# First expert blocks split among the pool chunks, norm sums two chunks at a time, third tile's rows turned behind the gather

## The chip, the core and the metric

The kernel runs on one core of one Trainium2 chip. The metric is the device time of one execution in microseconds (us). Four compute engines work beside one another, each in the order of its own program: PE (TensorE, matrix products, with the weight loads PEld beside them), DVE (VectorE), ACT (ScalarE) and POOL (GpSimd). SP issues most of the DMA transfers. They wait for one another on semaphores.

## The reference, cut to what matters

One inference step of a two-layer decoder over 280 tokens (16 meta tokens, 256 prompt tokens, 8 sample tokens), width 1024. Layer 0 is a state-space and sparse-attention mixer and a dense SwiGLU. Layer 1, where the change lies, is:

```python
def pool_mixer(u, hist, pos0, pool_w, pool_scale):      # windows 2, 4, 8, 16, one for each quarter of the channels
    ...
        mean = (cg - lagged)[:, n_hist:] / jnp.minimum(float(w), pos + 1.0)[None, :, None]
        pooled.append(mean - ext32[:, n_hist:, sl])
    mixed = jnp.einsum('bsgc,gcd->bsgd', pooled, pool_w.astype(f32)).reshape(B, S, D_MODEL)
    return (mixed * pool_scale.astype(f32)).astype(u.dtype), ext[:, T - POOL_HIST:]

def moe(h, router_w, w_gate, w_up, w_down):
    logits = (t @ router_w).astype(jnp.float32)
    top_v, top_i = lax.top_k(logits, TOP_K_EXPERTS)      # 2 of 8
    gates = jax.nn.softmax(top_v, axis=-1)
    ...
        out = out + dense_gate[:, e:e + 1] * swiglu(t, w_gate[e], w_up[e], w_down[e]).astype(jnp.float32)

def odd_layer(x, ...):
    y, new_hist = pool_mixer(rmsnorm(x, norm_mix), hist, pos0, pool_w, pool_scale)
    x = x + y
    x = x + moe(rmsnorm(x, norm_ffn), router_w, w_gate, w_up, w_down)
```

## The kernel before

The activations lie with channels on the partitions: 8 chunks (`c`) of 128 channels by 280 tokens (`x3` the residual, `h3` the normed rows). The program of every engine is written out by hand in this order: mixer, dense layer, **pool stage**, **router**, **gather**, and then a loop of passes, one for each expert (8 here, more if an expert has over 128 tokens).

**Pool stage.** DVE forms the sums over each window by doubling (L2215), two chunks at a time (group g = 0 to 3), writes mean minus token to `pl` (L2217 for the 272 prompt tokens, L2220 and L2221 for the first few, L2222 and L2223 for the 8 sample tokens) and counts `pooled`. PE multiplies each group by `pool_w` (L1233, two output chunks a group; each fp32 product is two records in the trace). DVE adds the result to the residual (`add_mixed`, L2205). ACT then scales the chunk by the next norm's weight into `h3` (L1707) and squares it into `sqs` (L1708). PE sums each chunk for the router's logits (L1217) and for the norm (L1221): that is `last_norm_sums`. Before, chunks 0 to 3 are summed after output chunk 5 of the pool product, and chunks 4 to 7 after chunk 7.

**Router.** ACT takes the root of the norm sums (`root(3)`, L1437) and copies the logits out (L1723). PE turns the rows of `h3` to tokens on partitions (`token_rows("h2n", ...)`, L1246), the norm (L1254) and the logits (L1259). DVE picks the two experts of a token (L2242 to L2265, which counts `picked`), and PE counts the rank of each token in its expert (L1267). DVE makes from it the selection matrices `pick` (L2281).

**Gather.** PE turns the residual's rows for the output (`token_rows("xn", ...)`, L1246, three token tiles of 128, 128 and 24; ACT copies each to `acc`, L1441), gathers the tokens of the first expert (L1277), fills two banks with zeros (`y`, L1302) and begins the passes.

**Expert weights.** A pass has 84 blocks of 128 x 1024. SP loads them in halves of 1 MB (two blocks) into `raw_w`. A block is split into a high part, copied by ACT (`high_part`, L1718), and a low part, subtracted by DVE (`low_part`, L2235), in one of 7 places. PE does three products a column range (L1322, L1326, L1327). ACT and DVE prepare blocks five ahead (`AHEAD`). Before the loop, ACT splits blocks 0 to 2 behind the root and 3 and 4 behind the router's rows; DVE subtracts blocks 0 and 1 (`FIRST_LOW = 2`) ahead of the router's arithmetic and 2 to 4 behind the gather. SP's half 7 waits for two low parts, half 8 for four, and so on.

PE's results go to seven banks in rotation (`fill_order` gives the order of fills, and so the bank of each); a fill waits until the last user of its bank has emptied it.

Of the kernel before, what the change touches and what calls it, by code (L numbers as in the profile page):

```python
# [24 lines left out]
P = 128  # L25
# [55 lines left out]
def shape_constants():  # L81
# [32 lines left out]
    for g, w in enumerate(WINDOWS):  # L114
        put("rw")[:, g * 16:g * 16 + w - 1] = 1.0 / np.arange(1, w, dtype=np.float32)
# [54 lines left out]
def fill_order():  # L170
# [33 lines left out]
    f += [("pool", c) for c in range(C)] + ["norm3"]  # L204
    f += ["router", ("h2n", 0, 0), ("h2n", 0, 1), "stdT", "routerT"] + [("h2n", t, i) for t in (1, 2) for i in range(2)]
    f += ["rank"] + [("xn", t, i) for t in range(TC) for i in range(2)]
# [76 lines left out]
FIRST_HIGH, FIRST_LOW = 3, 2  # L283
# [9 lines left out]
def hybrid_step(nc, a, o):  # L293

    with ExitStack() as ctx:
# [171 lines left out]
        win_a = tk(C * NP_).rearrange("p (c t) -> p c t", c=C)  # L467
        win_b = tk(C * NP_).rearrange("p (c t) -> p c t", c=C)
# [6 lines left out]
        ext = low[:, 2 * C * NP_:2 * C * NP_ + C * NB * 16].rearrange("p (c b r) -> p c b r", c=C, b=NB)  # L475
        pnew = low[:, FT * T + C * T + 2 * T:FT * T + C * T + 2 * T + D]
        assert 2 * C * NP_ + C * NB * 16 <= FT * T and D <= 4 * T
# [243 lines left out]
        def _(pool):  # L721
# [105 lines left out]
            for i in range(2):  # L827
                emptied(pool, ("xn", 2, i))
            nc.gpsimd.memset(pickTr[:, :].bitcast(F32), 0.0)
            nc.gpsimd.memset(ybr[:, :].bitcast(F32), 0.0).then_inc(sem("late_zeros"), 1)  # L830

        @block.tensor
        def _(pe):
# [367 lines left out]
            for i in range(2):  # L1201
                out = open_fill(("pnew", i))
                for q in range(4):
                    last = nc.tensor.transpose(out[0:23, q * P:(q + 1) * P], h3[:, 4 * i + q, T - 23:T], ident)
                last.then_inc(full(("pnew", i)), 1)
# [4 lines left out]
            def last_norm_sums(c0, c1):  # L1210
# [4 lines left out]
                for c in range(c0, c1):  # L1215
                    pe.wait_ge(sem("mixed_scaled"), c + 1)
                    last = mm(ps("router")[0:NE, 0:T], rw[:, c, :], h3[:, c, :], start=(c == 0), stop=(c == C - 1))  # L1217
                    if c == C - 1:
                        last.then_inc(full("router"), 1)
                    pe.wait_ge(sem("squares"), 3 * C + c + 1)  # L1220
                    last = mm(ps("norm3")[:, 0:T], ones, sqs[3][:, c, :], start=(c == 0), stop=(c == C - 1))  # L1221
                    if c == 0:

                        last.then_inc(sem("blocks_begun"), PLACES)
                    if c == C - 1:
                        last.then_inc(full("norm3"), 1)

            for co in range(C):
# [6 lines left out]
                last.then_inc(full(("pool", co)), 1)  # L1235
                if co == 5:
                    last_norm_sums(0, 4)
# [27 lines left out]
            for t in range(TC + 1):  # L1265
                for u in range(min(t + 1, TC)):
                    last = mm(out[:, t * NE:(t + 1) * NE], const("tri") if u == t else ones, sel[:, u, :],  # L1267
                              start=(u == 0), stop=(u == min(t, TC - 1)))
            last.then_inc(full("rank"), 1)
            token_rows("xn", x3, range(TC))  # L1270
# [23 lines left out]
            for half in range(2):  # L1294
                b = PASS_BANK[("gather", half)]
                pe.wait_ge(bank_free[b], BEFORE_FILL[b])
                gather_half(half, bank[b])
            pe.wait_ge(sem("late_zeros"), 1)
            for half in range(2):
                b = PASS_BANK[("y", half)]  # L1300
                pe.wait_ge(bank_free[b], BEFORE_FILL[b])
                mm(bank[b][:, :], yb3[:, 0, 0:P], yb3[:, 0, 0:512], start=True, stop=True).then_inc(bank_full[b], 1)  # L1302
# [117 lines left out]
        def _(act):  # L1420
# [284 lines left out]
            for c in range(C):  # L1705
                emptied(act, ("pool", c))
                A(h3[:, c, :], x3[:, c, :], ACT.Identity, scale=param("g_ffn1")[:, c:c + 1]).then_inc(sem("mixed_scaled"), 1)  # L1707
                A(sqs[3][:, c, :], x3[:, c, :], ACT.Square).then_inc(sem("squares"), 1)  # L1708
            root(3)

# [9 lines left out]
            for n in range(FIRST_HIGH):  # L1720
                high_part(0, n)
# [11 lines left out]
            for n in range(FIRST_HIGH, AHEAD):  # L1733
                high_part(0, n)
            act.wait_ge(sem("router_gap"), 1)
            A(g12[:, 1, :], g12[:, 0, :], ACT.Exp).then_inc(sem("router_exp"), 1)
            for t in range(TC):
                for i in range(2):
                    filled(act, ("xn", t, i))
                    n = TCN[t]  # L1740
                    copy_out(("xn", t, i), acc[0:n, t, i * 512:(i + 1) * 512], ps(("xn", t, i))[0:n, :])
            for half in range(2):
# [3 lines left out]
                  ACT.Copy).then_inc(sem("high_copied"), 1)  # L1746

# [64 lines left out]
        def _(dve):  # L1812
# [395 lines left out]
            for g, w in enumerate(WINDOWS):  # L2208
# [3 lines left out]
                for k in range(g + 1):  # L2212
                    dst, n = window_home(k)[:, cs, :], 1 << k
                    nc.vector.tensor_copy(dst[:, :, 0:n], src[:, :, 0:n])
                    link(TT(dst[:, :, n:NP_], src[:, :, n:NP_], src[:, :, 0:NP_ - n], ALU.add))  # L2215
                    src = dst
                link(STT(pl[:, cs, 0:NP_], win[:, cs, :], 1.0 / w, h3[:, cs, 0:NP_], ALU.mult, ALU.subtract))  # L2217

                few = const("rw")[:, g * 16:g * 16 + w - 1].unsqueeze(1).to_broadcast([P, 2, w - 1])
                link(TT(pl[:, cs, 0:w - 1], win[:, cs, 0:w - 1], few, ALU.mult))  # L2220
                link(TT(pl[:, cs, 0:w - 1], pl[:, cs, 0:w - 1], h3[:, cs, 0:w - 1], ALU.subtract))  # L2221
                link(nc.vector.tensor_reduce(pl[:, cs, NP_:T], ext[:, cs, :, 16 - w:16], AX.X, ALU.add))  # L2222
                STT(pl[:, cs, NP_:T], pl[:, cs, NP_:T], 1.0 / w, h3[:, cs, NP_:T], ALU.mult,  # L2223
                    ALU.subtract).then_inc(sem("pooled"), 1)
# [269 lines left out]
```

## Time and profile before

| | us |
|---|---|
| median of 3 runs | 1585.21 |
| lowest and highest run | 1580.08, 1591.72 |
| the profiled execution: its own time | 1590.82 |
| its span in the profile | 1588.7 |

Of the span PE is busy 97%, DVE 82%, ACT 62%, POOL 7%. A row of the time line gives start, busy time, engine, line, operation, output<-input, shapes and count, and in brackets how long the engine had been idle before it and what ended that. A row of the stretches gives the stretch, its length, the busy time of each engine in it with the number of instructions, TensorE's granted clock (1.00 is 2.4 GHz, 0.50 is 1.2 GHz), the DMA engines' busy share and GB/s.

### The profile page before, as it was taken

What the parts mean: (1) busy time and instruction counts of PE and PEld (TensorE: products, weight loads), DVE (VectorE), ACT (ScalarE), POOL (GpSimd) and SP (SyncE); (2) the same over time, 40 slices, a digit from 0 to 9 for tenths busy, and PEclk for the clock granted to TensorE, in tenths of its full rate; (3) what the DMA queues carried; (4) which work ended last, traced back from release to release, by engine and by line L of the source; (5) the groups of instructions that cost most, each with busy time, mean ns of one, the idle gap of its engine ahead of it and who ended that gap; (6) DMA issues with size and microseconds to landing.
All of it is one profiled execution on the core that took longest, in us unless ns stands there. A gap on an engine that the chain in (4) does not pass through costs nothing.

```text
span 1588.7 us, 23294 instructions
## 1 busy us (share of the span) xinstructions
PE 1537.4 (97%) x7624; PEld 1236.3 (78%) x7624; DVE 1299.2 (82%) x1729; ACT 992.1 (62%) x1302; POOL 110.8 (7%) x156
## 2 busy tenths in 40 slices
PE   6999899999998899999999999999999999999998
PEld 5665464999997578888888888888888888888886
DVE  8978883666644689889889889989989989988986
ACT  5121352544432467787787777777777778777774
POOL 1277600000000000000000000000000000000000
PEclk9998887999999899999999999999999999999999
DMA  6401244454464269989989989999998998999992
GB/s 230 160 27 54 66 160 128 154 177 159 127 182 172 106 221 362 380 307 358 374 315 357 365 319 355 370 341 329 360 357 323 366 364 307 366 371 327 345 363 89
DMA packets 212891, 420.83 MB, mean 265 GB/s; under 512 B 10233, under 2 KB 56469, under 8 KB 212572
## 3 DMA queue, kind: packets, MB, share of 16 engines
q1 hardware_dynamic: 211542, 414.37, 72.6%
q10 hardware_dynamic: 622, 3.45, 0.6%
q0 software_dynamic: 672, 2.32, 0.4%
q8 instruction: 30, 0.49, 0.1%
q14 instruction: 25, 0.20, 0.0%
HBM read 417.50 MB, written 3.07 MB: 265 GB/s over the span
## 4 chain that ended last, share of the span: by engine, by line
PE 85%; DVE 3%; ACT 1%; issue 1%; SPq 0%; DMA 0%; DVEq 0%; ACTq 0%
PE bank L1327 19%; PE bank L1322 19%; PE bank L1326 19%; PE bank L1176 3%; PE bank L1180 3%; PE bank L1179 3%; PE bank L1347 2%; PE bank L1191 1%; PE bank L1195 1%; PE bank L1194 1%; PE bank L885 1%; PE bank L1285 1%; PE bank L1362 1%; DVE split L2235 1%; PE bank L1233 1%
## 5 line engine op out<-in xcount | busy, mean ns | idle before, releaser
L2235 DVE TENSOR_TENSOR split<-raw_w,split 128x1024 fp32r<-128x1024 f32 x672 | 787.1, 1218 | 42.5 <-ACT split L1718 39.1
L1718 ACT ACTIVATE split<-raw_w 128x1024 fp32r<-128x1024 f32 x672 | 688.8, 1060 | 121.2 <-PE bank L1322 119.3
L1322 PE MATMUL bank<-split,xgr 128*128 128x512 f32 x896 | 358.1, 400 | 1.1 <-DVE xgr L2302 1.1
L1327 PE MATMUL bank<-split,xgr 128*128 128x512 f32 x896 | 354.2, 395 | 0.0
L1326 PE MATMUL bank<-split,xgr 128*128 128x512 f32 x896 | 354.1, 395 | 0.0
L1327 PEld LDWEIGHTS bank<-split,xgr 128*128 128x128 f32 x896 | 169.0, 189 | 39.8
L1322 PEld LDWEIGHTS bank<-split,xgr 128*128 128x128 f32 x896 | 169.2, 189 | 39.2 <-issue 1.5
L1326 PEld LDWEIGHTS bank<-split,xgr 128*128 128x128 f32 x896 | 169.1, 189 | 37.9
L1322 PE MATMUL bank<-split,hbr 128*128 128x512 f32 x448 | 178.0, 397 | 0.0
L1327 PE MATMUL bank<-split,hbr 128*128 128x512 f32 x448 | 177.0, 395 | 0.0
L1326 PE MATMUL bank<-split,hbr 128*128 128x512 f32 x448 | 176.8, 395 | 0.0
L1176 PE MATMUL bank<-split 128*128 128x280 f32 x352 | 102.8, 292 | 0.0
L1180 PE MATMUL bank<-split 128*128 128x280 f32 x352 | 102.5, 291 | 0.0
L1179 PE MATMUL bank<-split 128*128 128x280 f32 x352 | 102.1, 290 | 0.0
L1327 PEld LDWEIGHTS bank<-split,hbr 128*128 128x128 f32 x448 | 84.2, 188 | 19.9
L1326 PEld LDWEIGHTS bank<-split,hbr 128*128 128x128 f32 x448 | 84.3, 188 | 19.3
L1322 PEld LDWEIGHTS bank<-split,hbr 128*128 128x128 f32 x448 | 84.3, 188 | 19.3
L1661 ACT ACTIVATE split<-ring 128x1024 fp32r<-128x1024 f32 x44 | 46.6, 1059 | 65.5 <-PE bank L1176 65.5
L1784 ACT ACTIVATE late<-bank 128x512 f32<-128x512 f32 x56 | 33.5, 597 | 72.4 <-PE bank L1327 72.3
L2345 DVE TENSOR_TENSOR hbr<-bank,hbr 128x512 fp32r<-128x512 f32 x56 | 38.5, 688 | 49.0 <-ACT hbr L1761 48.9
L2143 DVE TENSOR_TENSOR split<-ring,split 128x1024 fp32r<-128x1024 f32 x44 | 53.9, 1225 | 19.2 <-ACT split L1661 19.2
L1176 PEld LDWEIGHTS bank<-split 128*128 128x128 f32 x352 | 66.3, 188 | 0.0
(429 smaller groups left out, 1993.1 us busy)
## 6 DMA issues: line engine op xcount, KB each, us to landing
raw_w<-in_moe_gate SPq DMA_DIRECT2D x112, 1024.0 KB, 5.5
raw_w<-in_moe_up SPq DMA_DIRECT2D x112, 1024.0 KB, 6.0
raw_w<-in_moe_down SPq DMA_DIRECT2D x112, 1024.0 KB, 5.7
ring<-in_w_gate SPq DMA_DIRECT2D x11, 1024.0 KB, 5.0
ring<-in_w_up SPq DMA_DIRECT2D x11, 1024.0 KB, 7.4
ring<-in_w_down SPq DMA_DIRECT2D x8, 1408.0 KB, 6.8
ring<-in_w_in SPq DMA_DIRECT2D x5, 2048.0 KB, 9.4
ring<-in_w_out SPq DMA_DIRECT2D x2, 2048.0 KB, 9.0
```

The source lines that it names most:

```text
L1176: first = mm(out[:, 0:T], w[0][:, c, :], dense_in(0, c), start=(c == 0), stop=False)
L1179: mm(out[:, 0:T], w[0][:, c, :], dense_in(1, c), start=False, stop=False)
L1180: last = mm(out[:, 0:T], w[1][:, c, :], dense_in(0, c), start=False, stop=(c == C - 1))
L1322: first = mm(out, hi, place[:, s, 0, cols], start=start, stop=False)
L1326: mm(out, lo, place[:, s, 0, cols], start=False, stop=False)
L1327: last = mm(out, hi, place[:, s, 1, cols], start=False, stop=stop)
L1661: A(place[:, n % FF_PLACES, 0, :].rearrange("p (c m) -> p c m", c=C), unit(name, 256)[:, k * C:(k + 1) * C, (f % 2) * P:(f % 2) * P + P], ...
L1718: A(place[:, s, 0, :], raw_w[:, at:at + BLOCK], ACT.Copy).then_inc(sem("high_ready"), 1)
L1784: A(th[:, j % 2, :], bank[b][:, :], ACT.Silu).then_inc(bank_free[b], 1)
L2143: TT(low_, unit(f"ffn{f // 2}", 256)[:, k * C:(k + 1) * C, (f % 2) * P:(f % 2) * P + P], high.bitcast(F32), ALU.subtract).then_inc(sem("ff ...
L2235: TT(place[:, s, 1, :], raw_w[:, at:at + BLOCK], place[:, s, 0, :].bitcast(F32), ALU.subtract).then_inc(sem("low_ready"), 1)
L2345: TT(dst, src, high.bitcast(F32), ALU.subtract).then_inc(bank_free[PASS_BANK[name]], 1)
```

## The change

Five things are altered, none of them inside the loop of passes:

1. DVE's pooling writes the sample tokens' sums into the window buffer and finishes prompt and sample tokens with one instruction; the table `rw` carries the factor `w` so that the first tokens need one small product.
2. The norm sums of chunks 0 and 1 follow output chunk 3, those of 2 and 3 follow chunk 5.
3. ACT splits blocks 0 to 2 ahead of chunk 2's scaling and blocks 3 and 4 ahead of chunk 4's; DVE subtracts four blocks, not two, ahead of the router's arithmetic.
4. The rank takes 7 products instead of 9.
5. The third tile's residual rows are turned behind the gather, ACT copies them behind the gather's copies, and the zero fill of the `y` banks reads the zeroed `pickTr` instead of `ybr`, so that POOL waits only for the norm.

```diff
-    f += [("pool", c) for c in range(C)] + ["norm3"]
-    f += ["router", ("h2n", 0, 0), ("h2n", 0, 1), "stdT", "routerT"] + [("h2n", t, i) for t in (1, 2) for i in range(2)]
-    f += ["rank"] + [("xn", t, i) for t in range(TC) for i in range(2)]
+    f += [("pool", c) for c in range(4)] + ["norm3", "router"] + [("pool", c) for c in range(4, C)]
+    f += [("h2n", 0, 0), "stdT", "routerT", ("h2n", 0, 1)] + [("h2n", t, i) for t in (1, 2) for i in range(2)]
+    f += ["rank"] + [("xn", 0, 0), ("xn", 0, 1), ("xn", 1, 0), ("xn", 2, 0), ("xn", 1, 1), ("xn", 2, 1)]
...
-FIRST_HIGH, FIRST_LOW = 3, 2
+FIRST_HIGH, FIRST_LOW = 3, 4
...
-            for i in range(2):
-                emptied(pool, ("xn", 2, i))
-            nc.gpsimd.memset(pickTr[:, :].bitcast(F32), 0.0)
-            nc.gpsimd.memset(ybr[:, :].bitcast(F32), 0.0).then_inc(sem("late_zeros"), 1)
+            emptied(pool, "norm3")
+            nc.gpsimd.memset(pickTr[:, :].bitcast(F32), 0.0).then_inc(sem("late_zeros"), 1)
...
+                if co == 3:
+                    last_norm_sums(0, 2)
                 if co == 5:
-                    last_norm_sums(0, 4)
+                    last_norm_sums(2, 4)
             last_norm_sums(4, C)
...
-            for t in range(TC + 1):
-                for u in range(min(t + 1, TC)):
-                    last = mm(out[:, t * NE:(t + 1) * NE], const("tri") if u == t else ones, sel[:, u, :],
-                              start=(u == 0), stop=(u == min(t, TC - 1)))
+            for u in range(TC):
+                mm(out[:, TC * NE:(TC + 1) * NE], ones, sel[:, u, :], start=(u == 0), stop=(u == TC - 1))
+            mm(out[:, 0:TC * NE], const("tri"), sel[:, :, :].rearrange("p t e -> p (t e)"), start=True, stop=False)
+            for u in range(TC - 1):
+                for t in range(u + 1, TC):
+                    last = mm(out[:, t * NE:(t + 1) * NE], ones, sel[:, u, :], start=False, stop=(u == TC - 2))
             last.then_inc(full("rank"), 1)
-            token_rows("xn", x3, range(TC))
+            token_rows("xn", x3, (0, 1))
...
+            token_rows("xn", x3, (2,))
             pe.wait_ge(sem("late_zeros"), 1)
             for half in range(2):
                 b = PASS_BANK[("y", half)]
                 pe.wait_ge(bank_free[b], BEFORE_FILL[b])
-                mm(bank[b][:, :], yb3[:, 0, 0:P], yb3[:, 0, 0:512], start=True, stop=True).then_inc(bank_full[b], 1)
+                for k in range(2):
+                    last = mm(bank[b][:, k * 256:(k + 1) * 256], pickTr[:, 0:P], pickTr[:, 0:256], start=True, stop=True)
+                last.then_inc(bank_full[b], 1)
...
+            for c in range(C):
+                if c == 2:
+                    for n in range(FIRST_HIGH):
+                        high_part(0, n)
+                if c == 4:
+                    for n in range(FIRST_HIGH, AHEAD):
+                        high_part(0, n)
+                emptied(act, ("pool", c))
+                A(h3[:, c, :], x3[:, c, :], ACT.Identity, scale=param("g_ffn1")[:, c:c + 1]).then_inc(sem("mixed_scaled"), 1)
+                A(sqs[3][:, c, :], x3[:, c, :], ACT.Square).then_inc(sem("squares"), 1)
+            root(3)
...
+            token_copies((0, 1))
             for half in range(2):
                 b = PASS_BANK[("gather", half)]
                 act.wait_ge(bank_full[b], BEFORE_FILL[b] + 1)
                 A(xg4[:, 0, 4 * half:4 * half + 4, :], bank[b][:, :].rearrange("p (c s) -> p c s", c=4),
                   ACT.Copy).then_inc(sem("high_copied"), 1)
+            token_copies((2,))
...
+                    if k == g:
+                        nc.vector.tensor_reduce(win[:, cs, NP_:T], ext[:, cs, :, 16 - w:16], AX.X, ALU.add)
                     link(TT(dst[:, :, n:NP_], src[:, :, n:NP_], src[:, :, 0:NP_ - n], ALU.add))
                     src = dst
-                link(STT(pl[:, cs, 0:NP_], win[:, cs, :], 1.0 / w, h3[:, cs, 0:NP_], ALU.mult, ALU.subtract))
...
-                link(TT(pl[:, cs, 0:w - 1], win[:, cs, 0:w - 1], few, ALU.mult))
-                link(TT(pl[:, cs, 0:w - 1], pl[:, cs, 0:w - 1], h3[:, cs, 0:w - 1], ALU.subtract))
-                link(nc.vector.tensor_reduce(pl[:, cs, NP_:T], ext[:, cs, :, 16 - w:16], AX.X, ALU.add))
-                STT(pl[:, cs, NP_:T], pl[:, cs, NP_:T], 1.0 / w, h3[:, cs, NP_:T], ALU.mult,
-                    ALU.subtract).then_inc(sem("pooled"), 1)
+                link(TT(win[:, cs, 0:w - 1], win[:, cs, 0:w - 1], few, ALU.mult))
+                STT(pl[:, cs, :], win[:, cs, :], 1.0 / w, h3[:, cs, :], ALU.mult, ALU.subtract).then_inc(sem("pooled"), 1)
```

How the order moves on PE in the pool stage (L1233, in the changed kernel L1230, is the pool product; L1217 the logits' sum and L1221 the norm's). Before:

```order
L1233 MATMUL bank<-low,ring 128x280 x12
L1217 MATMUL bank<-hT,params 8x280
L1221 MATMUL bank<-low,consts 128x280
L1217 MATMUL bank<-hT,params 8x280
L1221 MATMUL bank<-low,consts 128x280
L1217 MATMUL bank<-hT,params 8x280
L1221 MATMUL bank<-low,consts 128x280
L1217 MATMUL bank<-hT,params 8x280
L1221 MATMUL bank<-low,consts 128x280
L1233 MATMUL bank<-low,ring 128x280 x4
```

And with the change:

```order
L1230 MATMUL bank<-low,ring 128x280 x8
L1217 MATMUL bank<-hT,params 8x280
L1221 MATMUL bank<-low,consts 128x280
L1217 MATMUL bank<-hT,params 8x280
L1221 MATMUL bank<-low,consts 128x280
L1230 MATMUL bank<-low,ring 128x280 x4
L1217 MATMUL bank<-hT,params 8x280
L1221 MATMUL bank<-low,consts 128x280
L1217 MATMUL bank<-hT,params 8x280
L1221 MATMUL bank<-low,consts 128x280
L1230 MATMUL bank<-low,ring 128x280 x4
```

Two pairs of sums have moved from behind the third pool group to between the second and the third.

On PE from the rank to the passes. Before:

```order
L1267 MATMUL bank<-late,consts 128x8 x9
L1246 MATMUL bank<-consts,xT 128x128 x16
L1246 MATMUL bank<-consts,xT 24x128 x8
L1277 MATMUL bank<-pickr,hnr 128x128 x40
L1302 MATMUL bank<-ybr 128x512 x2
```

And with the change:

```order
L1265 MATMUL bank<-late,consts 128x8 x3
L1266 MATMUL bank<-late,consts 128x24
L1269 MATMUL bank<-late,consts 128x8 x3
L1245 MATMUL bank<-consts,xT 128x128 x16
L1278 MATMUL bank<-pickr,hnr 128x128 x40
L1245 MATMUL bank<-consts,xT 24x128 x8
L1305 MATMUL bank<-pickTr 128x256 x4
```

The eight transposes of the third tile now stand between the gather and the zero fills, and the rank is two products shorter.

On ACT from chunk 6 of the pool stage to the router's exponential. Before:

```order
L1707 ACTIVATE hT<-xT,params 128x280
L1708 ACTIVATE low<-xT 128x280
L1437 ACTIVATE low<-bank,small 128x280
L1718 ACTIVATE split<-raw_w 128x1024 x3
L1723 ACTIVATE late<-bank 8x280
L1731 ACTIVATE hnr<-bank,small 128x512 x4
L1731 ACTIVATE hnr<-bank,small 24x512 x2
L1718 ACTIVATE split<-raw_w 128x1024 x2
```

And with the change, from the second set of splits on (L1716; the first three stand two chunks further ahead; L1726 and L1727 scale and square a chunk, L1441 is the root, L1730 the copy of the logits):

```order
L1716 ACTIVATE split<-raw_w 128x1024 x2
L1726 ACTIVATE hT<-xT,params 128x280
L1727 ACTIVATE low<-xT 128x280
L1726 ACTIVATE hT<-xT,params 128x280
L1727 ACTIVATE low<-xT 128x280
L1726 ACTIVATE hT<-xT,params 128x280
L1727 ACTIVATE low<-xT 128x280
L1726 ACTIVATE hT<-xT,params 128x280
L1727 ACTIVATE low<-xT 128x280
L1441 ACTIVATE low<-bank,small 128x280
L1730 ACTIVATE late<-bank 8x280
```

All five splits now stand ahead of the root, and nothing stands between the root and the copy of the logits.

## Rows read from the trace of the kernel before

**Rows 1.** Stretches: a pass (PE, PEld, DVE, ACT, POOL, clock, DMA share, GB/s)

```profile
690.00:817.00 127.00, 127.00 (x569) 103.10 (x568) 113.74 (x114) 98.87 (x108) 0.00 (x0) 1.00 0.95 348
```

**Rows 2.** Waits of the DMA queue in the passes: us in total, times, longest

```profile
SPq L679 <- DVE split L2235: 816.4, 328, 19.7
```

**Rows 3.** Time line of PE, pool stage: start, busy, line, count, idle before

```profile
516.46 6.93 PE L1233 MATMUL bank<-low,ring 128*128 128x280 f32 x16 [0.85 <-DVE low L2223]
525.28 3.58 PE L1233 MATMUL bank<-low,ring 128*128 128x280 f32 x8 [1.89 <-DVE low L2223]
...
530.22 0.64 PE L1217 MATMUL bank<-hT,params 128*8 128x280 f32 x2
...
531.46 0.64 PE L1217 MATMUL bank<-hT,params 128*8 128x280 f32 x2
...
533.84 2.05 PE L1233 MATMUL bank<-low,ring 128*128 128x280 f32 x8
```

**Rows 4.** Time line of DVE, pool stage and router

```profile
514.77 0.72 DVE L2217 SCALAR_TENSOR_TENSOR low<-low,hT 128x544 f32<-128x544 f32 x1
515.53 0.16 DVE L2220 TENSOR_TENSOR low<-low,consts 128x2 f32<-128x2 f32 x1
...
516.14 0.17 DVE L2223 SCALAR_TENSOR_TENSOR low<-low,hT 128x16 f32<-128x16 f32 x1
...
542.35 2.36 DVE L2235 TENSOR_TENSOR split<-raw_w,split 128x1024 fp32r<-128x1024 f32 x2 [5.91 <-ACT split L1718]
...
545.21 0.17 DVE L2249 TENSOR_TENSOR late<-bank,small 128x16 f32<-128x16 f32 x1
...
552.29 0.18 DVE L2277 TENSOR_TENSOR late<-late,bank 128x24 f32<-128x24 f32 x1 [0.69 <-PE bank L1267]
...
552.91 0.68 DVE L2281 TENSOR_SCALAR pickr<-consts,late 128x128 fp32r<-128x128 f32 x3
```

**Rows 5.** Time line of ACT, pool stage and root

```profile
525.59 0.53 ACT L1707 ACTIVATE hT<-xT,params 128x280 f32<-128x280 f32 x1 [3.62 <-DVE xT L2205]
...
531.47 0.53 ACT L1707 ACTIVATE hT<-xT,params 128x280 f32<-128x280 f32 x1 [4.27 <-DVE xT L2205]
...
540.88 0.49 ACT L1437 ACTIVATE low<-bank,small 128x280 f32<-128x280 f32 x1 [3.55 <-PE bank L1221]
541.27 2.94 ACT L1718 ACTIVATE split<-raw_w 128x1024 fp32r<-128x1024 f32 x3
```

**Rows 6.** Time line of PE, from the norm's turn to the passes

```profile
541.64 0.73 PE L1254 MATMUL bank<-consts,low 1*128 1x1 f32 x6
...
548.92 3.34 PE L1267 MATMUL bank<-late,consts 128*128 128x8 f32 x18
...
552.11 4.96 PE L1246 MATMUL bank<-consts,xT 128*128 128x128 f32 x24
556.82 4.66 PE L1277 MATMUL bank<-pickr,hnr 128*128 128x128 f32 x40
561.32 0.68 PE L1302 MATMUL bank<-ybr 128*128 128x512 f32 x2
563.07 0.57 PE L1322 MATMUL bank<-split,xgr 128*128 128x512 f32 x1 [1.08 <-DVE xgr L2302]
...
570.98 1.41 PE L1285 MATMUL bank<-ybr,pickTr 128*128 128x512 f32 x4 [0.52 <-DVE ybr L2345]
```

**Rows 7.** Stretches, PE alone: busy, granted clock, DMA share, GB/s

```profile
521.50:522.00 0.50, 0.50 (x2) 0.50 0.04 12
...
525.80:529.20 3.40, 3.40 (x8) 0.50 0.00 0
...
549.60:556.50 6.90, 6.90 (x35) 0.51 0.00 1
556.50:563.20 6.70, 5.62 (x48) 1.00 0.01 2
563.30:566.70 3.40, 3.40 (x9) 0.51 0.11 17
```

More of the change, by code:

```diff
@@ L114, in shape_constants @@
     for g, w in enumerate(WINDOWS):
-        put("rw")[:, g * 16:g * 16 + w - 1] = 1.0 / np.arange(1, w, dtype=np.float32)
+        put("rw")[:, g * 16:g * 16 + w - 1] = w * (1.0 / np.arange(1, w, dtype=np.float32))
     put("hmask")[:] = (p[:, None] % H == np.arange(H)[None, :])
@@ L466, in hybrid_step @@
         tk, at = carve(low, 0)
-        win_a = tk(C * NP_).rearrange("p (c t) -> p c t", c=C)
-        win_b = tk(C * NP_).rearrange("p (c t) -> p c t", c=C)
+        win_a = tk(C * T).rearrange("p (c t) -> p c t", c=C)
+        win_b = tk(C * T).rearrange("p (c t) -> p c t", c=C)
         assert at[0] <= FT * T
@@ L474, in hybrid_step @@
         assert after + 12 * T + C * NB * 15 <= UT_AT + 4 * T
-        ext = low[:, 2 * C * NP_:2 * C * NP_ + C * NB * 16].rearrange("p (c b r) -> p c b r", c=C, b=NB)
+        ext = low[:, 2 * C * T:2 * C * T + C * NB * 16].rearrange("p (c b r) -> p c b r", c=C, b=NB)
         pnew = low[:, FT * T + C * T + 2 * T:FT * T + C * T + 2 * T + D]
-        assert 2 * C * NP_ + C * NB * 16 <= FT * T and D <= 4 * T
+        assert 2 * C * T + C * NB * 16 <= FT * T and D <= 4 * T
         token_rs = rinv[:, 0:4]
@@ L1204, in _ @@
                     last = nc.tensor.transpose(out[0:23, q * P:(q + 1) * P], h3[:, 4 * i + q, T - 23:T], ident)
+                    if i == 0 and q == 0:
+                        last.then_inc(sem("blocks_begun"), PLACES)
                 last.then_inc(full(("pnew", i)), 1)
@@ L1221, in last_norm_sums @@
                     last = mm(ps("norm3")[:, 0:T], ones, sqs[3][:, c, :], start=(c == 0), stop=(c == C - 1))
-                    if c == 0:
-                        last.then_inc(sem("blocks_begun"), PLACES)
                     if c == C - 1:
@@ L1704, in _ @@
             act.dma_start(o["pool_s"][:, 14, :], pnew[15:23, :]).then_inc(sem("pool_out"), 16)
[L1705 to L1709, printed above, removed]
             def high_part(i, n):
@@ L1718, in high_part @@
                 A(place[:, s, 0, :], raw_w[:, at:at + BLOCK], ACT.Copy).then_inc(sem("high_ready"), 1)
-            for n in range(FIRST_HIGH):
-                high_part(0, n)
+            for c in range(C):
[9 more added lines that the diff above has]
+            root(3)
             filled(act, "router")
@@ L1732, in _, with token_copies @@
                       scale=token_rs[0:n, t:t + 1]).then_inc(sem("hn_high"), 1)
-            for n in range(FIRST_HIGH, AHEAD):
-                high_part(0, n)
             act.wait_ge(sem("router_gap"), 1)
             A(g12[:, 1, :], g12[:, 0, :], ACT.Exp).then_inc(sem("router_exp"), 1)
[L1737 to L1741, printed above, removed]
+            def token_copies(ts):
+                for t in ts:
+                    for i in range(2):
+                        filled(act, ("xn", t, i))
+                        n = TCN[t]
+                        copy_out(("xn", t, i), acc[0:n, t, i * 512:(i + 1) * 512], ps(("xn", t, i))[0:n, :])
+            token_copies((0, 1))
             for half in range(2):
```

## The prediction

> **What bounds the kernel now.** I read the stretches of the passes first. In a pass PE is busy 127.00 of 127.00 us at the granted clock 1.00 [rows 1], and SP's queue waits for DVE's low parts, not the reverse: 816.4 us in 328 waits [rows 2]. Eight passes are PE's own work and the change leaves their code alone, so whatever it moves lies between the pool stage and the first blocks of the first pass, some 55 us. Read next the time lines of PE, DVE and ACT there. In the pool stage PE starts at 516.46 when DVE's first group is ready, is done with two groups and then idle for 1.89 us before the third [rows 3]; from 525.28 it has no gap until the norm sums end at 540.85 (ACT's root starts at 540.88, after 3.55 us of waiting for PE [rows 5]). From there DVE's arithmetic leads, from its first product of logits at 545.21 to the rank at 552.29 and `pick` at 552.91 [rows 4]. Then PE leads again: 24 turned tiles, 40 gather products, two zero fills and the first pass's products at 563.07 [rows 6]. PE's granted clock falls to the lower level (1.2 GHz) after short gaps: 525.8 to 529.2, 549.6 to 556.5 and 563.3 to 566.7; the gather ran at the full level (2.4 GHz) [rows 7].
>
> **Pool stage.** A group ends with four small or large instructions: from 514.77 to 516.31 in the first group, 1.54 us [rows 4]. Now it is a small product (0.16 and its hand-over, about 0.2) and one instruction of 560 instead of 544 elements (about 0.75), and the reduction (under 0.2 here) lies unlinked before the last doubling: 1.54 - 0.95 - 0.1 = 0.49 saved, so PE starts at 515.97. The other three groups save about as much, and only the third's counts: it is ready at about 524.2 (before: 525.1).
> PE's two groups take 6.93 [rows 3], to 522.9. Chunk 0's and 1's sums follow. A chunk costs 1.24 us at the full clock (530.22 to 531.46 [rows 3]): 2.5 us, to 525.4, in a place where PE was idle 1.89. The third group finds its data there. At the full clock it takes 1.95 (the fourth group's row, 2.05 with the overlap [rows 3]), against 3.58 before: the gap after which the clock fell is filled, so I take the full clock. That is 527.3. Sums of chunks 2 and 3 to 529.8, the fourth group to 531.8, four more chunks to 536.8. Against 540.85 the norm ends **4.0 us earlier**. Should the third group run at the lower level still, it is 2.4.
> What hides ACT's five splits (4.9 us at 2.94 for three [rows 5]): ACT idled 3.62 before chunk 2 and 4.27 before chunk 4 [rows 5]. The first three run from 521.5 to 524.5, chunk 2 is ready at about 524.7; the next two from 526.5 to 528.5, chunk 4 at about 530. Were that cover gone, each split would delay the sums by 1 us, 5 in all. Their weights have come: the DMA engines fall from full to 0.04 busy at 521.5 [rows 7].
>
> **Root to logits.** Before: 540.88 to 545.21, 4.33 us [rows 4, 5]. ACT's logits copy stood behind 2.94 us of splits, DVE's first reciprocal behind two low parts (2.36 from 542.35 [rows 4]). Without them PE's turn of the norm ends the wait: it ends at 542.37 [rows 6], 1.5 after the root's start, and 0.45 of reciprocals and hand-over follow, with the logits' copy and turn (0.4 and 0.3) beside and just behind. I take 2.1: **2.2 saved**. DVE's four low parts (4 x 1.18) now start when the last chunk is added, at 532.3, and end at 537.0, 1.3 before the norm's turn. They open SP's halves 7 and 8 some 10 us sooner, in a stretch in which nothing else is loaded; POOL's zeros of `hnr` follow the last pool product, also earlier. Both cost nothing. Without that cover half a low part, 0.6, would show.
>
> **Logits to gather.** DVE's choice of experts and PE's start of the rank move along unchanged. The rank is 18 records in 3.34 us [rows 6], now 14: 3.34 x 4/18 = **0.7 saved**. 8 of 24 turned tiles leave: 4.96 x 8/24 = **1.65 saved** [rows 6]. This is PE's path; DVE's own reaches `pick` at 553.6 (552.91 and 0.68 [rows 4]), and since DVE's six low rows then end just before the rank (it waited 0.69 for it [rows 4]) that path saves 4.0 + 2.2 + 0.65, to 546.8, while PE's ends at 557.0 - 8.55 = 548.5. PE's still ends last, by 1.7. If PE had the full clock in rank and turns it would wait for `pick` at 546.8: 10.2 saved there instead of 8.55.
>
> **Behind the gather.** Before, PE ended the gather at about 561.4, filled zeros (0.68), idled 1.08 and began at 563.07 [rows 6], waiting for ACT's and DVE's second half. Now 8 turns of the third tile (1.25 to 1.65) and four short fills (0.7) come first, then the load of the pass count: 2.5 us after the gather where it was 1.6, **0.9 lost** (ends: 0.6 and 1.7, the 1.08 left whole). The turns fill the wait only in part and push the rest out.
> First pass: DVE has one low part left there, not three, 2.36 less [rows 4], so the 0.52 wait before the first scatter [rows 6] goes: **0.5 saved**. ACT's two copies of the third tile put its `y` copies 1.1 us later, under DVE's tables. Nine of the first products ran at the lower level, about 0.43 apart against 0.23, 3.4 us of it [rows 7]: 1.7 us to be had if the shorter gap leaves the clock up, 0 if not. Half, **0.8**.
>
> **Sum.** 4.0 + 2.2 + 0.7 + 1.65 - 0.9 + 0.5 + 0.8 = 8.95, say 9. Against the profiled execution's 1590.82 that is 1581.8. This execution is 5.6 above the median of the three runs (1585.21), so as a median: **1576**.
>
> The clock terms come from rows: the level fell with gaps of 1.89, some 2 and 1.08 us around it [rows 3, 6, 7]. The Trainium skill, page "TensorE: Matmul & The Clock Gate", section "Part 1: The HAM clock gate", has the clock fall only after a longer idle spell than any of these three, and rise under sustained activity. By that rule these short gaps would cost no clock, so filling them would give none back, and the sum would be 9 - 1.6 - 0.8 = 6.6; the trace disagrees. The page also says that the gate runs by itself, so that the same kernel meets it at other places from run to run; one profile can't show that. It speaks for the first rival below, whose price comes from rows.
>
> **Rivals.**
> *A, the gather at the lower clock (0.18).* Before, 4.96 us of turned tiles stood ahead of the gather and the level rose at 556.5, just before it [rows 6, 7]. Now a third of them is gone. For: the level came only at the end of the run. Against: the gap before the rank is the same and may fall otherwise. Price: 40 products at half rate, up to 4.4 us more, and up to 1 more in turns. 9 - 4.5 = 4.5 saved: 1581.
> *B, the passes take it back (0.10).* The DMA engines are 0.95 busy in a pass [rows 1]. If weights were the bound, an earlier start would only move the wait. Against: SP's queue waits for DVE [rows 2], PE never idles. 1585.
> *C, ACT late in the pool stage (0.06).* If its splits start late or the weights lag, chunk 2's scaling and all sums behind it slip; half of the cover gone, 2.5 us: 1579.
> *D, slower (0.04).* PE stays at the lower level from the first moved sums to the passes, because the work is now interleaved. Eight chunks' sums at twice 1.24 (+9.9), third group as before (the 1.6 gone), fourth +1.6, gather +4.4, the rest of the first four blocks +2.9: 20.4 against 9, net 11 slower, 1597. It decides once PE is at the lower level for more than about half of that work; against it, the level rose after 3.4 us of dense products at 529.2 [rows 7].
> The forecast has the rest, 0.62.
>
> **Range and chances.** The forecast's own ends are 12 saved (PE's full clock at the rank and at the first pass, 1573) and 6 saved (third group at the lower level and the hand-over dear, 1579). A and B reach to 1585. The three runs before lie 11.6 apart, 5 to 6.5 on either side of their median, which a new median may share in part: I widen to 1568 and 1587. One per cent, 16 us, is what a measurement tells from no change. A saving of 16 is beyond every case and needs the runs' scatter: 0.07. Slower by 16 needs more than D: 0.03. Within: 0.90.
>
> **What would show it.** In the changed profile: no PE gap between second and third pool group, and the third group in 2 us, not 3.6; the root starting near 537; the logits' first product 2.1 after it; a gather that starts near 548.5 and takes 4.4 us; the first pass's products 2.5 us behind the gather. A gather of 6 us or more is A. PE gaps inside a pass are B. A wait of PE for ACT's scaled chunks is C. The sum is wrong if the root starts later than 538.5, or if DVE's low parts end behind the norm's turn.

## The result and the profile after

| | before | changed |
|---|---|---|
| median, lowest to highest of 19 runs, us | 1588.22, 1580.08 to 1591.72 | 1580.78, 1570.86 to 1583.84 |
| the profiled execution's span, us | 1588.7 | 1576.5 |

The ratio of the runs is 0.9946, 95% interval 0.9932 to 0.9961: the change makes the kernel some 0.5% faster, 7.4 us between the medians. The forecast was 9 us. The median that it gave, 1576, lies 4.8 us below the measured 1580.78: 3.0 of that is the median before, 1588.22 here against 1585.21 in the three runs that the forecast had, and the rest is the smaller saving. The two spans lie 12.2 apart, more than the medians; the profiles of the experiments show how far two spans can differ.

A pass is as before; the stretches of the changed kernel (columns as in [rows 1]):

```profile
681.60:808.60 127.00, 127.00 (x569) 103.09 (x568) 113.37 (x113) 98.88 (x108) 0.00 (x0) 1.00 0.95 348
```

The time line of PE in the changed kernel's pool stage (L1230 is the pool product), to be laid beside [rows 3]:

```profile
516.33 5.52 PE L1230 MATMUL bank<-low,ring 128*128 128x280 f32 x16 [0.32 <-DVE low L2232]
521.78 0.64 PE L1217 MATMUL bank<-hT,params 128*8 128x280 f32 x2
...
524.18 2.12 PE L1230 MATMUL bank<-low,ring 128*128 128x280 f32 x8
...
529.51 0.71 PE L1230 MATMUL bank<-low,ring 128*128 128x280 f32 x2 [0.73 <-DVE low L2232]
```

The 1.89 us gap is gone, the third group takes 2.12 instead of 3.58, and there is a new wait: PE idles 0.73 us until DVE has the fourth group. The first two groups are shorter too, 5.52 us instead of 6.93 [rows 3]: the granted clock is low until about 519.4 here, and was until about 522.4. DVE's and ACT's time lines, beside [rows 4, 5]:

```profile
532.10 4.62 DVE L2243 TENSOR_TENSOR split<-raw_w,split 128x1024 fp32r<-128x1024 f32 x4
536.68 0.08 DVE L2248 MEMSET late<- 128x24 f32 x1
538.23 0.17 DVE L2250 RECIPROCAL small<-bank 128x2 f32<-128x2 f32 x1 [1.48 <-PE bank L1253]
...
538.67 0.18 DVE L2257 TENSOR_TENSOR late<-bank,small 128x16 f32<-128x16 f32 x1
...
545.10 0.18 DVE L2285 TENSOR_TENSOR late<-late,bank 128x24 f32<-128x24 f32 x1
```

```profile
521.30 2.94 ACT L1716 ACTIVATE split<-raw_w 128x1024 fp32r<-128x1024 f32 x3
524.49 0.53 ACT L1726 ACTIVATE hT<-xT,params 128x280 f32<-128x280 f32 x1 [0.25 <-DVE xT L2215]
...
525.99 1.99 ACT L1716 ACTIVATE split<-raw_w 128x1024 fp32r<-128x1024 f32 x2
529.82 0.53 ACT L1726 ACTIVATE hT<-xT,params 128x280 f32<-128x280 f32 x1 [1.84 <-DVE xT L2215]
...
536.63 0.49 ACT L1441 ACTIVATE low<-bank,small 128x280 f32<-128x280 f32 x1 [3.55 <-PE bank L1221]
```

Both sets of splits fit in ACT's idle time (0.25 and 1.84 us of it are left), and DVE's four low parts end 1.48 us before PE's turn of the norm. At 545.10 DVE goes from its own low rows to the rank without a wait. PE from there on, beside [rows 6]:

```profile
547.00 4.66 PE L1278 MATMUL bank<-pickr,hnr 128*128 128x128 f32 x40
551.50 1.04 PE L1245 MATMUL bank<-consts,xT 128*24 128x128 f32 x8
552.29 0.72 PE L1305 MATMUL bank<-pickTr 128*128 128x256 f32 x4
553.25 0.49 PE L1326 MATMUL bank<-split,xgr 128*128 128x512 f32 x1 [0.25 <-DVE xgr L2310]
```

The stretches of PE alone, columns as in [rows 7]:

```profile
521.80:528.60 6.80, 6.80 (x25) 1.00 0.01 2
543.20:546.70 3.50, 3.50 (x19) 0.51 0.00 0
547.00:551.50 4.50, 4.50 (x43) 1.00 0.02 5
553.20:558.90 5.70, 5.64 (x24) 1.00 0.00 0
```

From its start the gather is followed by the first pass after 6.25 us, exactly as before: turns and fills take the place of most of the idle 1.08 us, and 0.25 of it is left. Of the three low stretches that stood behind the second pool group [rows 7], one of 3.5 us is left. And the first pass's 24 products run at the full level with no wait before the scatter.

### The profile page after: what moved, and what is told of

Same layout as the page of the kernel before. It is cut to its first block, busy times and chain, and to the rows that moved or that the text cites. A ratio compares the mean times of both kernels' runs of the same rounds, so it can differ in the third digit from the quotient of the medians.

```text
span 1576.5 us, 23279 instructions
## 1 busy us (share of the span) xinstructions
PE 1528.1 (97%) x7622; PEld 1230.3 (78%) x7622; DVE 1297.2 (82%) x1721; ACT 991.4 (63%) x1302; POOL 109.1 (7%) x155
## 4 chain that ended last, share of the span: by engine, by line
PE 85%; DVE 3%; ACT 1%; issue 1%; SPq 0%; DMA 0%; DVEq 0%
PE bank L1331 19%; PE bank L1330 19%; PE bank L1326 19%; PE bank L1174 3%; PE bank L1178 3%; PE bank L1177 3%; PE bank L1351 2%; PE bank L1189 1%; PE bank L1193 1%; PE bank L883 1%; PE bank L1192 1%; PE bank L1286 1%; PE bank L1366 1%; PE bank L1110 1%; PE bank L1154 1%
## 5 line engine op out<-in xcount | busy, mean ns | idle before, releaser
L2243 DVE TENSOR_TENSOR split<-raw_w,split 128x1024 fp32r<-128x1024 f32 x672 | 787.1, 1218 | 36.6 <-ACT split L1716 32.6
L1716 ACT ACTIVATE split<-raw_w 128x1024 fp32r<-128x1024 f32 x672 | 688.2, 1060 | 118.5 <-PE bank L1326 116.6
L1326 PEld LDWEIGHTS bank<-split,xgr 128*128 128x128 f32 x896 | 168.8, 188 | 37.9 <-issue 0.4
L1665 ACT ACTIVATE split<-ring 128x1024 fp32r<-128x1024 f32 x44 | 46.6, 1059 | 65.5 <-PE bank L1174 65.5
```

The lines of the kernel that those rows point to most:

```text
L1326: first = mm(out, hi, place[:, s, 0, cols], start=start, stop=False)
L1665: A(place[:, n % FF_PLACES, 0, :].rearrange("p (c m) -> p c m", c=C), unit(name, 256)[:, k * C:(k + 1) * C, (f % 2) * P:(f % 2) * P + P], ...
L1716: A(place[:, s, 0, :], raw_w[:, at:at + BLOCK], ACT.Copy).then_inc(sem("high_ready"), 1)
L2243: TT(place[:, s, 1, :], raw_w[:, at:at + BLOCK], place[:, s, 0, :].bitcast(F32), ALU.subtract).then_inc(sem("low_ready"), 1)
```

## Experiments

Each kernel was timed in five rounds beside the kernel before on the same chip. The first four experiments below were timed together on one chip, the next four (router gap, pool wait, both, before with its gap filled) on another and the last four (both filled again, splits back with gaps filled, pooling back, rank back) on a third. Besides the ratio, every profile gives the same six times: the starts of the root of the last norm, of DVE's first product of logits, of PE's gather, of the first pass and of its fifth block (block 4), counted from the start of DVE's reciprocal of the third norm, just ahead of the pool stage; and the rest, from block 4 to the end of the span. In us:

| kernel | root | logits | gather | pass | block 4 | rest | ratio to before (95%) |
|---|---|---|---|---|---|---|---|
| before | 32.6 | 37.0 | 48.6 | 54.8 | 64.0 | 1016.5 | |
| changed | 28.0 | 30.0 | 38.4 | 44.6 | 51.5 | 1016.4 | 0.9946 (0.9932 to 0.9961) |
| changed, again | 27.9 | 29.9 | 38.7 | 49.8 | 57.1 | 1015.3 | 0.9938 (0.9918 to 0.9957) |
| norm sums back | 29.4 | 31.4 | 39.4 | 48.5 | 55.0 | 1016.4 | 0.9964 (0.9948 to 0.9980) |
| splits back | 27.9 | 32.2 | 42.2 | 53.4 | 61.7 | 1016.4 | 0.9999 (0.9983 to 1.0015) |
| turns back | 27.8 | 29.8 | 40.4 | 47.0 | 53.8 | 1016.5 | 0.9944 (0.9924 to 0.9963) |
| router gap filled | 27.9 | 29.9 | 37.9 | 44.2 | 51.1 | 1016.5 | 0.9931 (0.9908 to 0.9954) |
| pool wait filled | 27.1 | 29.2 | 37.2 | 43.8 | 50.7 | 1016.5 | 0.9929 (0.9906 to 0.9952) |
| both filled | 27.1 | 29.2 | 37.2 | 43.5 | 50.3 | 1016.4 | 0.9926 (0.9902 to 0.9949) |
| both filled, again | 28.1 | 30.1 | 38.1 | 44.4 | 51.3 | 1016.5 | 0.9929 (0.9907 to 0.9951) |
| before, gap filled | 31.0 | 35.3 | 45.3 | 51.6 | 60.7 | 1016.5 | 0.9996 (0.9978 to 1.0014) |
| splits back, gaps filled | 28.4 | 32.8 | 40.8 | 49.9 | 58.4 | 1016.4 | 0.9962 (0.9946 to 0.9979) |
| pooling back | 30.0 | 32.1 | 40.1 | 46.4 | 53.2 | 1016.5 | 0.9953 (0.9934 to 0.9972) |
| rank back | 27.9 | 29.9 | 39.5 | 46.6 | 53.4 | 1016.4 | 0.9944 (0.9924 to 0.9964) |

Each row is one profile, except that the ratio comes from all its runs. The rest is the same within 1.2 us in all: the passes take nothing back and give nothing. The reciprocal itself starts at 500.7 to 510.2 us of the span in these profiles, whatever the kernel: much of the scatter of the runs arises ahead of the stage that was changed.

**The changed kernel again** (no edit).

> The changed kernel once more, unaltered, as the yardstick of this chip. Work theory (the gain is work taken off the path that ends the stage, the same in every execution): root about 4.2 us earlier, logits' first product 2.3 us nearer to the root, gather start 3.3 us nearer, in the profile again; ratio to the kernel before 0.995. Clock theory (most of the profile's 12 us is where the clock happened to fall): the profile shows another sum, between 7 and 12 us, with the difference in stretches of granted clock 0.50; the ratio is the same 0.995.

Measured: ratio 0.9938. Up to the gather it is the same profile to 0.3 us. The gather is not:

```profile
545.36 8.78 PE L1278 MATMUL bank<-pickr,hnr 128*128 128x128 f32 x40
553.94 1.91 PE L1245 MATMUL bank<-consts,xT 128*24 128x128 f32 x8
```

```profile
517.60:541.20 23.60, 20.97 (x101) 1.00 0.48 173
541.30:558.20 16.90, 16.90 (x78) 0.50 0.01 1
```

40 products take 8.78 us instead of 4.66, in a stretch in which the rows show PE busy all the time and the granted clock is 0.50. That is the first rival of the prediction, in the same kernel that did not show it in the other profile. Up to the start of the gather the work theory holds; from there to block 4 the same program took 13.1 us in one execution and 18.4 in the other.

**Norm sums back.**

```diff
-                if co == 3:
-                    last_norm_sums(0, 2)
                 if co == 5:
-                    last_norm_sums(2, 4)
+                    last_norm_sums(0, 4)
```

> The changed kernel with the norm sums of chunks 0 to 3 together behind output chunk 5, as before; all else as changed. Work theory: PE idles some 2.2 us ahead of the third pool group and the two chunks' sums (2.5 us) come behind it; root start against the third norm's root 1.4 us later than in the changed kernel. Clock theory: the gap also lets the clock fall, the third group takes 3.6 us and not 2.1, root 3 us later.

```profile
524.74 2.13 PE L1230 MATMUL bank<-low,ring 128*128 128x280 f32 x8 [2.33 <-DVE low L2230]
```

Root 1.4 us later, as the work theory has it. A gap of 2.33 us stands before the third group and the clock did not fall after it: a gap of that length did not lower it every time. In the runs the loss is 3.8 us between the medians (1581.62 and 1577.80), more than the 1.4 of the path, with intervals that overlap; this profile's gather ran in part at 0.50.

**Splits back** (ACT's five `high_part` behind the root and behind the router's rows, and no longer among the chunks; `FIRST_LOW = 2`).

```diff
-FIRST_HIGH, FIRST_LOW = 3, 4
+FIRST_HIGH, FIRST_LOW = 3, 2
...
             root(3)
+            for n in range(FIRST_HIGH):
+                high_part(0, n)
```

> The changed kernel with ACT's five splits behind the root and behind the router's rows, and DVE's two low parts ahead of the router, as before. Work theory: root start unchanged, the logits' first product 4.3 us behind the root's start and not 2.0 (2.3 us lost), and 0 to 0.5 us of wait before the first scatter: 2.3 to 2.8 us slower in all. Rival (the splits were hidden and DVE's choice of experts or PE sets the end anyway): under 0.5 us slower.

The path is as expected: logits 4.3 behind the root, 2.3 lost. But the kernel lost all that the change had gained: its median is 1587.76 us, the changed kernel's in the same rounds 1577.80 and the kernel before's 1587.62. Its profile:

```profile
540.67 0.37 PE L1258 MATMUL bank<-consts,late 8*128 8x8 f32 x3 [2.25 <-ACT late L1726]
```

```profile
540.10:563.50 23.40, 22.32 (x104) 0.50 0.14 46
```

The clock is low from PE's wait for the copy of the logits (2.25 us) until into the first pass, and the gather takes 8.8 us. Both theories I had for this kernel were too small for the 10 us; it led to the filled gaps.

**Turns back** (`token_rows("xn", x3, (0, 1, 2))` ahead of the gather and ACT's copies with it).

> The changed kernel with the third tile's rows turned and copied ahead of the gather, as before. As predicted (turns ahead cost 1.65, behind they cost 0.9 of it again): 0.8 us slower. As the changed profile reads (the first pass began 1.6 us behind the gather in both, so behind the gather the turns were free): 1.0 to 1.6 us slower. Clock theory: PE's gap behind the gather is again over 1 us, the clock falls with it and the first 9 products take 0.43 us apart: up to 3.4 us slower.

```profile
547.61 1.49 PE L1245 MATMUL bank<-consts,xT 128*24 128x128 f32 x6
548.75 5.01 PE L1278 MATMUL bank<-pickr,hnr 128*128 128x128 f32 x40
553.60 0.68 PE L1304 MATMUL bank<-pickTr 128*128 128x256 f32 x4
555.36 0.50 PE L1325 MATMUL bank<-split,xgr 128*128 128x512 f32 x1 [1.07 <-DVE xgr L2308]
```

The gather starts 1.7 to 2.0 us later and the 1.07 us gap behind it is back. Against the changed kernel's first profile the first pass and block 4 come 2.3 us later, more than the 1.0 to 1.6: the turns are 2.0 of it, and the gather, whose start still ran at the lower level, takes 5.01 us instead of 4.66. The clock theory's part missed: after the 1.07 us gap the clock did not fall, and the first products ran at the full level. In the timing (0.9944 against 0.9938 in the same rounds) no difference shows.

**Idle products on PE.** These kernels add products of constants that no result uses, into a bank that is overwritten afterwards. The one for the router's gap, ahead of the last turned rows:

```diff
+                if i == 1:
+                    for _k in range(2):
+                        mm(filler[:, 0:512], ones, consts[:, 0:512], start=True, stop=True)
                 out = open_fill(("h2n", 2, i))
```

> The changed kernel with two more products on PE (128 x 512, fp32, constants only, into the bank that the rank overwrites) in the 1.9 us in which PE waits ahead of the last turned rows and the rank. No result uses them. Clock theory (that gap lets the clock fall, and then rank, turns and in some executions the gather run at the lower level): the granted clock stays 1.00 from the pool stage to the passes, rank in 1.6 us, gather in 4.5 us in every execution, gather start bound by the selection matrices; block 4 of the first pass at 51 us after the third norm's reciprocal; median 3 to 5 us below the changed kernel's, ratio to the kernel before 0.990 to 0.992. Work theory: no wait is taken away, so no difference to the changed kernel, ratio 0.994.

> The changed kernel with six such products in the 6 us in which PE waits for the norm ahead of the pool stage. Clock theory: the first two pool groups run at the full level, 3.9 us and not 5.5 to 6.9; the root starts 0.5 to 1 us earlier (from there DVE's fourth group sets the pace), the rest as the changed kernel, with the gather at the lower level in some executions: ratio 0.993 to 0.994. Work theory: no difference, or a loss of some tenths of a us where the last of the six overhangs.

> The changed kernel with both sets of idle products. Clock theory: both gains, median 4 to 6 us below the changed kernel's, ratio 0.989 to 0.991, and runs that scatter less (under 6 us between lowest and highest, not 12). Work theory: no difference to the changed kernel.

```profile
505.60:556.00 50.40, 45.55 (x230) 1.00 0.46 172
```

This is both sets together: no low level from the third norm to the first pass. With the router's gap filled the rank, the turns and the gather ran at the full level (the gather in 4.65 us), and PE then waits 1.07 us for the selection matrices, so that DVE sets the start of the gather. With the wait before the pool stage filled, the first two groups take 2.12 us each, not 5.5 together, and the root comes 0.75 earlier. The gain over the changed kernel is smaller than forecast and not shown: the ratios 0.9931, 0.9929 and 0.9926 lie just below the interval of the changed kernel's 0.9946 (0.9932 to 0.9961) and inside that of its second timing (0.9918 to 0.9957), and all the intervals overlap. The three scatter little, 3.1, 3.1 and 4.3 us between lowest and highest of 6 runs, against 13 in 19 runs and 8.2 in 8 runs of the changed kernel. That is no evidence for the clock theory: turns back, with nothing filled, lies within 4.3 us in 7 runs, and rank back within 2.9 in 6.

> The changed kernel with both sets of idle products once more. Clock theory: no stretch below 1.00 from the third norm to the passes, block 4 of the first pass within 0.5 us of the first profile of it (50.3 us after the reciprocal), where two profiles of the changed kernel stood at 51.5 and 57.1; runs again within 6 us of one another, ratio to the kernel before 0.990 to 0.993. Rival (the first profile of it was luck): block 4 anywhere between 50 and 57.

Block 4 at 51.3, 1 us from the first profile of it, so outside the 0.5 that was expected: here the clock fell for 3.5 us in the first pool groups in spite of the filled wait. It was at the full level from 519.2 on:

```profile
519.20:558.00 38.80, 36.53 (x200) 1.00 0.29 106
```

Its runs lie 6.2 apart. This version is the fastest measured here, but its intervals, 0.9902 to 0.9949 and 0.9907 to 0.9951, overlap the changed kernel's; that it beats it isn't shown.

**The kernel before with its pool gap filled.**

> The kernel before with two such products in PE's 1.9 us gap between the second and the third pool group (where the change puts two chunks' norm sums). Clock theory: the third group takes 2.0 us, not 3.6, the root starts 1.6 us earlier, all without any work moved; median 0 to 2 us below the kernel before. Work theory: nothing gained, root where it was.

```profile
522.65 1.88 PE L1239 MATMUL bank<-consts 128*128 128x512 f32 x4
524.86 2.12 PE L1233 MATMUL bank<-low,ring 128*128 128x280 f32 x8 [0.32 <-DVE low L2227]
...
559.38 0.49 PE L1326 MATMUL bank<-split,xgr 128*128 128x512 f32 x1 [1.08 <-DVE xgr L2306]
...
567.28 1.40 PE L1289 MATMUL bank<-ybr,pickTr 128*128 128x512 f32 x4 [2.08 <-DVE ybr L2349]
```

The third group takes 2.12 us, not 3.58, and the root comes 1.6 us earlier with no work moved: the price of the clock in that place, as the clock theory gave it. In the timing it does not show (0.9996, and the interval holds both no gain and the 1.6).

This profile also answers for the first blocks. The 1.08 us gap behind the gather is there as before, but the clock stays up, and still the first pass needs 9.1 us to block 4, as before: PE now waits 2.08 us for DVE instead of 0.52. With three low parts left behind the gather DVE sets that time, and the clock alone gains nothing there.

**Splits back, with both gaps ahead of the rank filled.**

> The changed kernel with the splits where they were before (as in the earlier run without them moved), and idle products on PE (128 x 512, two in each) in the two gaps that this leaves ahead of the rank: the wait for the copy of the logits and the wait for the first low rows. Clock theory (the moved splits gained 2.2 us of path, and the rest of their 9 us by taking away a PE gap in which the clock fell): the granted clock stays 1.00 to the passes, the gather takes 4.5 us, the first product of logits is still 4.3 us behind the root, block 4 of the first pass at 53 to 54 us after the third norm's reciprocal; 2 to 3 us slower than the changed kernel with its router gap filled, ratio to the kernel before 0.994 to 0.996. Work theory (the splits' place itself costs 9 us): ratio 1.000 again.

```profile
551.00 6.94 PE L1292 MATMUL bank<-pickr,hnr 128*128 128x128 f32 x40 [1.09 <-DVE pickr L2301]
```

```profile
522.60:553.00 30.40, 28.18 (x144) 1.00 0.24 81
553.00:559.60 6.60, 6.60 (x33) 0.50 0.02 4
```

The ratio is 0.9962 against 0.9999 without the fills: of the 0.6% that putting the splits back cost, the idle products return 0.4%, and the intervals don't overlap (0.9946 to 0.9979, 0.9983 to 1.0015). No work was moved, so that part was clock. The rest against the changed kernel's 0.9938, 0.2% or some 4 us, holds the 2.3 us of path; the intervals overlap and tell no more. The profile missed its expectation: the clock, up until 553.0, fell in the middle of the gather. Filling the gap ahead of the rank makes the low level rarer, not impossible: of the four profiles with it filled one has a low stretch between rank and passes, of the eight without (the changed kernel twice, norm sums, splits, turns, pooling and rank back, pool wait filled) seven have, all but pooling back.

**Pooling back** (DVE's arithmetic of before) and **rank back** (nine products).

> The changed kernel with the pooling arithmetic of before on DVE. Work theory: each group 0.5 us longer; PE starts the pool stage 0.5 us later, and since in the changed kernel PE waits 0.7 us for the fourth group, all four count: root 2 us later, 2 us slower in all. Rival (as predicted, where only the first group and the third were on the path): 0.5 to 1 us.

> The changed kernel with the rank in nine products as before. At the full clock the rank ends before DVE's six low rows do, and the turns before the selection matrices: 0 us. At the lower level it is on PE's path: 0.4 to 0.8 us later. In the timing under 0.8 us slower, not to be told from none.

```profile
523.61 2.13 PE L1230 MATMUL bank<-low,ring 128*128 128x280 f32 x8 [0.87 <-DVE low L2233]
```

Pooling back: the row is the fourth group, for which PE waits 0.87 us; the root comes 2.1 us later. All four groups count; in the profile the work theory holds and the prediction's reading, that only the start and the third group count, falls. The ratio, 0.9953, can't be told from the changed kernel's. Rank back: the gather starts 0.9 to 1.2 later, somewhat over the 0.4 to 0.8 expected, with rank and turns at the lower level; 0.9944 can't be told from the changed kernel's own ratio either.

## Why the prediction came out right, and where it was off

The total, 9 us forecast and 7.4 measured, is right; its parts were not all. In the first profile of the changed kernel the parts add to 12.5 us, 3.5 over the forecast, in the second to 6.9. That the medians' 7.4 lies so near 9 is in part luck: most parts were forecast too small, and rival A, a loss that was left out of the sum, takes 5 us back in the second profile. How much of it the medians hold stays open.

- **Pool stage**, forecast 4.0, measured 4.6 and 4.7 [rows 3, 5]. That only the third group's readiness counts was wrong. With two chunks' sums moved into PE's gap, PE catches up and waits for DVE's fourth group (0.73 us), so that all four shortened groups lie on the path: 2.1 us by the pooling back, against 0.5. It holds there although the first two groups took 6.99 us, as before. In the changed kernel they took 5.52 and 5.41, a saving of clock that the working, with 6.93, didn't have, and of which the wait for the fourth group leaves half. The sums themselves are worth 1.4, the clock in the third group 1.6 (before, gap filled); taken one at a time the three add to 5.1 against 4.6 in all, so they overlap.
- **Root to logits**, forecast 2.2 saved, measured 4.33 to 2.04, 2.3. The cover of DVE's low parts was 1.48 us, forecast 1.3. Splits back confirms the size. What no term had: with the splits behind the root PE also waits for the copy of the logits, 2.16 to 2.25 us, and in splits back the clock fell in that gap, ahead of rank and gather.
- **Logits to gather**, forecast 2.35 saved, measured 11.6 to 8.3 and 8.7, 3.3 and 2.9. In the first profile the turns gave what was forecast, 4.7 to 3.0 us. The rank gave twice its 0.7: from its start to the turns 3.2 us before and 1.8 now, at the full clock for its first half, where the working had scaled a rank at the lower level. The low stretch was 3.5 us long, against 6.9 before [rows 7].
- **Behind the gather**, forecast 0.9 lost, measured nothing lost. The working put the turns (1.25 to 1.65), the fills and the load of the pass count one behind the other, 2.5 us. Turns and fills took 0.8 and 0.7 from start to end, no time of the load shows, and all of it ran beside ACT's and DVE's 1.6 us [rows 6].
- **First blocks**, forecast 1.3 saved, measured 2.3 and 1.9: the wait of 0.52 is gone, and most or all of the nine slow products. The prediction added the two as separate gains. They are one: in the kernel before with its gap filled the slow products are gone and nothing is gained, because DVE's three low parts then set the time. By these rows it takes the two low parts moved forward (2.36 us less for DVE) for the clock to be worth anything here. That the shorter gap kept the clock up isn't shown, since after gaps of 1.07 and 1.08 us it stayed up in two other profiles (turns back; before, gap filled).
- **Rival A, the gather at the lower clock**, had 0.18. The whole gather ran low in one of the two profiles of the changed kernel and in splits back, much of it in norm sums back and in splits back with gaps filled (7.12 and 6.94 us), a small part in turns back, rank back and pool wait filled (5.01 to 5.46). In the changed kernel its price was 4.9 us from the gather's start to the first pass, forecast up to 4.4 and 1 more for the turns. This is why the two profiles lie 12.5 and 6.9 us ahead of the kernel before at block 4, on both sides of the medians' 7.4. As one mechanism beside the sum it was under-weighted: it is a state that executions of one and the same kernel may meet or not, and a median may hold a share of it. The two profiles of the kernel before (one with its gap filled) have the gather at the full level. How often each kernel meets it can't be told from one or two profiles.
- **Rivals B, C and D** did not occur: the rest is 1015.3 to 1016.5 us in every profile, PE has no wait for ACT in the pool stage, and in both profiles of the changed kernel the clock was up from within the second pool group to the rank.

Of the page "TensorE: Matmul & The Clock Gate" of the Trainium skill two statements (section "Part 1: The HAM clock gate") can now be weighed. That the gate runs by itself, so that one kernel meets it in other places from run to run: the traces agree (5.3 us between two profiles of one program from the gather's start). That it takes an idle spell longer than these gaps for the clock to fall: they disagree, as the prediction said: with splits back and gaps filled it fell at 553.0 us, 2 us into a gather in which the rows show PE never idle, with 1.09 us of waiting ahead of it.

## What to carry to other kernels

Before a short stage between two dense ones is priced, look at the granted clock row by row: moving work into a gap of PE may be worth as much by the clock that it keeps as by the work (1.6 and 1.4 us here), and with the splits behind the root filling two waits of PE with products that nobody uses won back 0.4%, some 6 us. When a wait is filled, ask which engine then ends last; here the pooling on DVE became worth four times its forecast, and in the first pass a faster PE only waited longer for DVE. And one profile of a stage with such gaps is one draw: take two before a difference of a few us is read from spans.

## What the runs showed of the hardware

- 40 products of 128 columns behind one another took 4.66 us at the granted clock 1.00 and 8.78 at 0.50, with PE busy throughout by the rows; in the second case (the changed kernel again) the low level lasted 16.9 us without an idle spell in the rows, from the rank through turns, gather and fills, and ended only in the first pass's products.
- The level did not always fall with a gap: after 2.33 us it stayed up in one profile (norm sums back), after 1.89 it fell in another [rows 3, 7]; after 1.08 it fell in the kernel before [rows 6, 7] and stayed up in the same place with the pool gap filled. And it fell once 2 us into a gather without a gap (splits back, gaps filled).
- Two idle products in a gap of 1.9 us cost nothing (router gap filled): the turned rows behind them started 0.18 us after them, when DVE's row came.
